# Squared-relu groups: t2 chained in PSUM on b11, every product added straight into the output quadrants

## What is computed

```
def sq_relu_mlp(h, w_up, w_down):
    return jnp.square(jax.nn.relu(h @ w_up)) @ w_down
```

## Time and profile before

| what | value |
|---|---|
| median of 3 runs | 1903.17 us (1901.72 to 1905.87) |
| span of the profiled execution | 1900.5 us; its own time is not given apart |
| TensorE, weight loads, VectorE, ScalarE, GpSimd busy | 1890.5, 1555.8, 1339.4, 985.3, 95.3 us |
| groups of layer 0 | begin at 270.1, 351.7, 433.3 us |
| groups of layer 1 | begin at 757.3, 838.9, 920.5 us |

### The profile page before, as it was taken

How to read it: one execution, slowest core, us unless ns; L and a number is a source line. 1 busy time by engine, 2 the same in 40 slices (tenths; PEclk the granted TensorE clock), 3 DMA queues, 4 the chain that set the end, 5 groups by cost and what they waited for, 6 DMA issues and landing times. The chain is left out here.

```text
span 1900.5 us, 25399 instructions
## 1 busy us (share of the span) xinstructions
PE 1890.5 (99%) x9486; PEld 1555.8 (82%) x9486; DVE 1339.4 (70%) x1988; ACT 985.3 (52%) x1587; POOL 95.3 (5%) x114
## 2 busy tenths in 40 slices
PE   9999999999999999999999999999999999999999
PEld 8877888887888778888888988667788888888887
DVE  7656665656566766665566788998897867767867
ACT  5634464544546746454444435788445446545454
POOL 0100000101000000000100000000000000100101
PEclk9999999999999999999999999999999999999999
DMA  7632156757323114756752356222224634644735
GB/s 230 155 100 94 73 142 180 166 162 202 123 79 144 46 56 132 201 139 173 180 162 67 112 143 167 89 90 78 89 91 143 166 89 155 155 148 118 199 95 122
DMA packets 69676, 249.79 MB, mean 131 GB/s; under 512 B 7730, under 2 KB 7986, under 8 KB 68916
## 3 DMA queue, kind: packets, MB, share of 16 engines
q1 hardware_dynamic: 55728, 198.88, 31.0%
q0 software_dynamic: 13824, 49.29, 14.8%
q10 hardware_dynamic: 4, 0.00, 0.0%
HBM read 246.05 MB, written 2.10 MB: 131 GB/s over the span
## 5 line engine op out<-in xcount | busy, mean ns | idle before, releaser
L545 PE MATMUL ps<-HH,WH 128*128 128x512 f32 (+1 forms) x1696 | 626.2, 369 | 0.9 <-ACT AT L1736 0.9
L547 PE MATMUL ps<-HH,WL 128*128 128x512 f32 (+1 forms) x1696 | 621.2, 366 | 0.0
L546 PE MATMUL ps<-HL,WH 128*128 128x512 f32 (+1 forms) x1696 | 620.9, 366 | 0.0
L1299 ACT ACTIVATE WH<-WR 128x1024 fp32r<-128x1024 f32 x333 | 348.9, 1056 | 479.8 <-PE ps L547 315.3
L2030 DVE TENSOR_TENSOR WL<-WR,WH 128x1024 fp32r<-128x1024 f32 (+1 forms) x332 | 403.1, 1218 | 263.1 <-ACT WH L1299 262.4
L545 PEld LDWEIGHTS ps<-HH,WH 128*128 128x128 f32 x1696 | 319.9, 189 | 62.5 <-issue 11.6
L547 PEld LDWEIGHTS ps<-HH,WL 128*128 128x128 f32 x1696 | 319.9, 189 | 52.2
L546 PEld LDWEIGHTS ps<-HL,WH 128*128 128x128 f32 x1696 | 320.0, 189 | 50.7
L959 PE MATMUL ps<-WH,AH 128*128 128x512 f32 x490 | 191.0, 390 | 0.4 <-DVE WL L2030 0.4
L960 PE MATMUL ps<-WH,AL 128*128 128x512 f32 x490 | 190.7, 389 | 0.0
L961 PE MATMUL ps<-WL,AH 128*128 128x512 f32 x490 | 190.6, 389 | 0.0
(11 more groups left out here) (386 smaller groups left out, 2606.9 us busy)
## 6 DMA issues: line engine op xcount, KB each, us to landing
WR<-in_up SPq DMA_DIRECT2D x96, 512.0 KB, 4.2
WR<-in_quart SPq DMA_DIRECT2D x60, 512.0 KB, 3.6
WR<-in_quart POOLq DMA_DIRECT2D x48, 512.0 KB, 6.3
WR<-in_in SPq DMA_DIRECT2D x48, 512.0 KB, 3.6
WR<-in_down SPq DMA_DIRECT2D x16, 512.0 KB, 3.5
WR<-in_quartf SPq DMA_DIRECT2D x14, 512.0 KB, 3.5
WR<-in_quartf POOLq DMA_DIRECT2D x14, 512.0 KB, 5.6
MT<-in_up SPq DMA_DIRECT2D x12, 512.0 KB, 4.1
```

The source lines that it names most:

```text
L545: e.matmul(ps, wh, hi[:, c, cols], start=c == 0, stop=False)
L546: e.matmul(ps, wh, lo[:, c, cols], start=False, stop=False)
L547: y = e.matmul(ps, wl, hi[:, c, cols], start=False, stop=c == x.n - 1)
L1299: e.activation(x.wh[:, 0:n], raw(m, x.raw)[:, 0:n], AF.Copy).then_inc(*k.mark("whi", u))
```

## The change

The product t2 is no longer a sum of its own: its first matmul doesn't clear the banks of b11 (which VectorE has read by then) but goes on adding, so that the banks hold b11 + t2. Each product is added into, or subtracted from, every quadrant that it belongs to, at the place in VectorE's list where its one operation was. The three accumulators in PX, `partial` and the seven combinations are gone. The first writer of a quadrant in a layer copies and waits for the last transpose that read MT. The extra buffers of the plain part are released by the last tile of group 2.

```diff
-        add(f"down{layer}3", down, extra=m.EXTRA["mlp"], freed=("sum7", layer, 6))
+        add(f"down{layer}3", down, extra=m.EXTRA["mlp"], freed=("unit", at[f"seven{layer}2"] + 13))
...
-    m.PX = arena("PX", [128, 3, 2, 512], 59)
...
+M_BANKS = {"b11": 0, "b21": 2, "t1": 4, "b22": 6, "t2": 0, "t3": 2, "t4": 4}
+M_STARTS = ("b11", "b21", "t1", "b22", "t3", "t4")
+M_PARTS = {"b11": (((0, 0), 1),), "b21": (((0, 0), 1),), "t1": (((0, 1), 1), ((1, 1), 1)), "b22": (((0, 1), 1),),
+           "t2": (((0, 1), -1), ((1, 1), -1), ((1, 0), 1)), "t3": (((1, 1), -1), ((1, 0), 1)), "t4": (((1, 0), 1),)}
...
-            y = pairs(j, h, b, f, v, h == 0 and not (last and what in ("t2", "t3")), h == 1)
+            y = pairs(j, h, b, f, v, h == 0 and not (last and what in ("t2", "t3")) and not (chained and what not in M_STARTS), h == 1)
...
-        if o == 0:
-            e.tensor_copy(acc, src).then_inc(*k.mark("part", layer, o, what))
-        else:
-            e.wait_ge(*k.on("part", layer, o - 1, what))
-            e.tensor_tensor(acc, src, acc, A.add).then_inc(*k.mark("part", layer, o, what))
-
-    def together(n):
...
+        for to, sign in M_PARTS[what]:
+            acc = quarter(m, *to)
+            if to not in prior:
+                e.wait_ge(*k.on("turned", f"mlp{layer}", 3, 1))
+                if sign > 0:
+                    e.tensor_copy(acc, src).then_inc(*k.mark("part", layer, o, what, to))
+                else:
+                    e.tensor_scalar(acc, src, -1.0, None, A.mult).then_inc(*k.mark("part", layer, o, what, to))
+            else:
+                e.wait_ge(*k.on("part", *prior[to]))
+                if sign > 0:
+                    e.tensor_tensor(acc, src, acc, A.add).then_inc(*k.mark("part", layer, o, what, to))
+                else:
+                    e.tensor_tensor(acc, acc, src, A.subtract).then_inc(*k.mark("part", layer, o, what, to))
+            prior[to] = (layer, o, what, to)
+        k.also("part", layer, o, what)
...
                 if j:
                     plain(24 + j - 1)
-                    together(j - 1)
```

More of the change, by code:

```diff
@@ L385, in quarter @@
     return m.MT[:, 2 * i:2 * i + 2, 512 * j:512 * j + 512]
[L388 to L392, removed]
 def mixes(m, key):
@@ L948, in t_seven @@
     u, stream = k.at[name], stream_of(name)
-    last = name == "sevenf2"
+    last, chained = name == "sevenf2", key in (0, 1)
     def pairs(j, h, b, f, v, start, stop):
@@ L958, in pairs @@
             e.wait_ge(*k.on("side", key, 4 * o + p, SIDE_PART[f]))
-            e.matmul(m.ps[b + v], xh, x.wh[:, w], start=start and q == 0, stop=False, skip_group_check=last)
-            e.matmul(m.ps[b + v], xl, x.wh[:, w], start=False, stop=False, skip_group_check=last)
-            y = e.matmul(m.ps[b + v], xh, x.wl[:, w], start=False, stop=stop and q == n - 1, skip_group_check=last)
+            e.matmul(m.ps[b + v], xh, x.wh[:, w], start=start and q == 0, stop=False, skip_group_check=last or chained)
+            e.matmul(m.ps[b + v], xl, x.wh[:, w], start=False, stop=False, skip_group_check=last or chained)
+            y = e.matmul(m.ps[b + v], xh, x.wl[:, w], start=False, stop=stop and q == n - 1, skip_group_check=last or chained)
         return y
     for j, (what, h) in enumerate(stream):
-        b, f = (LAST_BANKS if last else SEVEN_BANKS)[what], SIDE[what]
+        b, f = (LAST_BANKS if last else M_BANKS if chained else SEVEN_BANKS)[what], SIDE[what]
         e.wait_ge(*k.on("wlo", u + j))
@@ L2428, in v_mlp @@
     post, then = ("post_mlp0", "mix1") if layer == 0 else ("post_mlp1", "in2")
+    prior = {}
     def others(p):
@@ L2444, in part @@
         u = at[f"seven{layer}{o}"] + STREAM.index((what, 1))
-        src, acc = pair(m, SEVEN_BANKS[what]).rearrange("p (a f) -> p a f", a=2), partial(m, what)
+        src = pair(m, M_BANKS[what]).rearrange("p (a f) -> p a f", a=2)
         e.wait_ge(*k.on("unit", u))
-        if o == 0:
-            e.tensor_copy(acc, src).then_inc(*k.mark("part", layer, o, what))
-        else:
-            e.wait_ge(*k.on("part", layer, o - 1, what))
-            e.tensor_tensor(acc, src, acc, A.add).then_inc(*k.mark("part", layer, o, what))
-    def together(n):
[L2455 to L2460, removed]
+        for to, sign in M_PARTS[what]:
[14 more added lines that the diff above has]
+        k.also("part", layer, o, what)
     def ups(o):
```

## The result

| | kernel before | changed kernel |
|---|---|---|
| median of 20 runs each | 1903.32 us | 1907.72 us |
| lowest to highest | 1901.72 to 1905.87 | 1903.25 to 1909.62 |
| span of the profiled execution | 1900.5 us | 1905.0 us (its own time 1906.76) |

The ratio is 1.0021, with a 95% interval of 1.0014 to 1.0027: slower by 4.4 us in the medians. The prediction was 3.8 us and 1907.0 us.

A forecast was written before the change was run, and what follows sets the result against it. TensorE, 99% busy at full clock, bounds the kernel; VectorE work costs only before a late cut. Waits of 1.87, 1.68, 0.20 and 0.06 us sum to 3.8, added to the 1903.17 median: 1907.0 us, range 1902.0 to 1910.5.

The forecast's parts named there:

- Pieces and their price: On VectorE: 10 more operations over two layers at 1.135 us each, 11 us more, hidden unless before a late cut.
- The term, t2 in front of u14's cut: Two added VectorE operations per group delay the subtraction preparing the first up tile behind it by 2.27 us, costing 3.8 us.
- Its size by group: Waits at the first up tile: layer 0's groups 0.20, nothing, 1.87 us; layer 1's 0.06, nothing, 1.68 us.
- under 0.3 us behind the others: Sign: new first-up-tile waits stay under 0.3 us, except 1.6 to 1.9 us behind each layer's last group.
- the second rival: More groups wait at the first up tile because transfers land later: 1910.5, up to 1914.4 us; chance 0.10.
- a later u13: Counter-sign: a group's last weight tile (second of t4) itself starting later would make the forecast wrong; no size given.
- a longer wait at u10: Expected sign: no wait longer than before at a group's first t3 weight tile.
- Costed at nothing: The listed parts of the change, in the groups and the last up stage, were each taken to cost or gain nothing.
- Cover: Rival: t4's second tile normally lands 1.9 us sooner, leaving room at the first up tile: no cost, 1903.2 us; chance 0.20.
- Catching up: Rival: TensorE makes up the first up tile's wait in the next tiles: 1903.2 us; chance 0.05.
- The combinations: Rival: those removed from the last up stage were on the path, returning up to 15.9 us: 1891 us; chance 0.07.
- a fall of the clock after a wait of 1.9 us: Counter-sign: TensorE's clock falling below 1.000 after such a wait at the first up tile would make the forecast wrong.

The follow-up runs named there:

- e1: Changed kernel with the cut of the first up tile (u14) moved ahead of t2's three operations: 1903.57 us, ratio 1.0001 to the kernel before.
- e2: Changed kernel with t2 added into one quadrant only, its other two operations left out: 1903.32 us, ratio 1.0002 to the kernel before.
- e5: Kernel before with two copies of t2's banks into an unused buffer behind t2's one operation: 1908.09 us, ratio 1.0021.
- e3: Changed kernel with each layer's gain fetch moved behind the third up tile after the layer's last group: 1903.77 us, ratio 1.0000 to the kernel before.
- e9: Changed kernel with one more copy of t2's banks behind t2's three operations: 1915.67 us (five runs), ratio 1.0065 to the kernel before.
- e6: Kernel before without the seven combinations of each layer, extra buffers released by the last tile of group 2: 1902.93 us, ratio 0.9998.
- e4: Changed kernel with two more copies of t2's banks behind t2's three operations: 1928.03 us (four runs), ratio 1.0125 to the kernel before.
- e7: Kernel before with each layer's gain fetch moved behind the third up tile after the layer's last group: 1901.67 us, ratio 0.9991.

## Why the prediction was right

- **Pieces and their price.** Right. VectorE does 11.3 us more; additions and copies take 1218 ns, the subtractions 1214. Operations in a row start 1.135 us apart in the profile after, and four of them take 4.54 us, not 4.9. The plain rule of the Trainium skill ("VectorE: DVE Perf Modes", section "The DRAIN you can't avoid"), that the next operation does not start until the pipeline is empty, would have made the sum 4.5 us; it does not describe these rows, while the section's own exception, an operation that is not held, would fit them. That the median loss is 4.4 is no support for the plain rule.
- **The term, t2 in front of u14's cut.** Right in place and mechanism. Moving the cut (e1) or leaving out two operations (e2) takes the loss away, and two copies a group that compute nothing, put into the kernel before (e5), make it.
- **Its size by group.** G2 and G5 were put at 1.87 and 1.68 and came 1.81 us late each. G3 was put at 0.06 and lost nothing. G0 was put at 0.20 and came 1.11 late, so one of the prediction's signs, under 0.3 us behind the others, was not met: the summed t4 tile landed later there (u13's cut starts at 303.96; the same cut in the kernel before started at 302.61, and TensorE itself was only 0.43 us later at the group's start). That is a small part of the second rival, and e3 and e9 show other groups in G0's place. The prediction took each group's room from one execution as if it were fixed.
- **What the sum left out.** The lateness at u13 of G2, 1.46 us before (470.16 less 433.34 and 13 tiles of 2.72), is 0.76 after (470.92 less 434.80 and the same): 0.70 less. A reason that fits is that TensorE reaches the group 1.46 us later, while the transfers need not be later by as much; it was not tested. On the other side u13 of G5 is 0.29 us late where it was in time, with a wait of 0.20 at u10 that was not there before, and TensorE begins G0 0.43 later. The prediction had named a later u13 and a longer wait at u10 as signs against itself; both are there in G5, and small. With the 0.09 us that each of three first tiles gives back, the profiled executions come out: 4.73 - 0.70 + 0.29 + 0.43 - 0.27 = 4.5 us, which is the difference of the spans. So the term at u14 was 0.9 us short, nearly all of it G0, and what the sum left out comes to -0.25 us: that these terms nearly cancel is luck; the place, the mechanism and the size at G2 and G5 are not.
- **Costed at nothing: t1, t3, b21, chaining, the transposes' wait, SyncE, GpSimd, the combinations.** Right as far as can be measured, together by e2 and e1, the combinations and the release apart by e6.
- **The rivals.** Cover did not come: u14 was late by 1.81 us behind both G2 and G5, and even with the gain fetch moved (e3) it waits 2.1 us in all. Catching up is excluded: the first tile behind the new waits takes 5.35 us instead of 5.44, so 0.09 of 1.9 comes back. The combinations were not on the path (e6).
- **The clock.** The prediction named a fall of the clock after a wait of 1.9 us as a sign against it. There was none: the granted clock is 1.00 from 475.5 to 480 and from 963.2 to 968 us, behind both waits. The mean of 0.999 comes from a stretch of 0.50 behind TensorE's last instruction (1902.8 on). Waits of 2.65 us and more did bring it down (e4, e9).

## What to carry to other kernels

Where one engine is full and another prepares its operands, price an added operation by what stands right behind it in its engine's list and by how much room that has, not by the engine's load: here two more operations a group cost 4.4 us in front of a cut that came late in three groups of six, and four more a group cost nothing measurable behind it. Put the preparation of the next operand ahead of the clearing up of the last result. And take the room from several executions: here the landing of one tile moved it by 1 to 3 us between the profiles.

## What the runs showed of the hardware that was not expected

The cost of a wait of TensorE had a step. In the timelines of e4 and e9 waits up to 2.42 us cost their length; those of 2.65, 3.05, 3.07 and 4.20 us (twice) came with a granted clock of 0.50 for about 3.4 us, once 6.8 (481.4 to 488.1 in e4), and a first tile 1.5 to 2.6 us longer than behind the short waits. In e4 the clock was down before the wait had ended, in e9 it fell 0.6 to 0.7 us after. What a wait between 2.42 and 2.65 us does was not measured.

So e4's two more copies a group cost 20.3 us over the change in the medians, and 19.6 in the spans of the profiled executions (1924.6 less 1905.0). Of the 19.6, the longer waits at the first up tiles are 12.0, the clock 5.6, and the waits inside the groups, 3.2 us instead of 1.3, another 1.9.

A 1 MB fetch of gains in the middle of a group, for a use more than 90 us later (536.06 us in the kernel before), held up GpSimd's accumulating transfers: the one issued 1.4 us behind it in G2 took 10.8 us to land in the kernel before and 5.4 without the fetch (e7), and in G5 10.1 and 5.4. By which part of the way they hinder each other is not shown.
